# A two-layer transformer trunk on one core: the second exchange of hidden blocks is issued behind the third weight load of the next up projection

## The reference

```python
def squared_relu_mlp(x, w1, w2):
    h = jax.nn.relu(x @ w1)
    return (h * h) @ w2
...
        x = layer_norm(ALPHA * x + mix, ln_mix_g[layer], ln_mix_b[layer])
        x = layer_norm(ALPHA * x + squared_relu_mlp(x, mlp_w1[layer], mlp_w2[layer]), ln_mlp_g[layer], ln_mlp_b[layer])
```

## Time and profile before

| what | value |
|---|---|
| runs | 2122.4, 2122.74, 2124.38 us |
| profiled execution: its own time | 2122.97 us |
| its span, first to last instruction | 2121.2 us |
| granted TensorE clock, mean | 0.999 |
| busy: PE, DVE, ACT, POOL | 2098.9, 1596.4, 1055.1, 25.6 us |
| groups `pair_step(0)` to `(5)`, of about 85 us each | from about 474 us (layer 0) and 1551 us (layer 1) |
| HBM read | 406.26 MB, 193 GB/s over the span |

### The profile page before, as it was taken

The page is one execution under the profiler, slowest core; times in us unless marked ns, Lnnn a source line. Parts: engine busy times, 40 slices in busy tenths (PEclk is TensorE's granted clock), DMA queues, the critical chain, the costliest instruction groups (busy, mean ns, idle before and its releaser), DMA issues.

```text
span 2121.2 us, 26630 instructions
## 1 busy us (share of the span) xinstructions
PE 2098.9 (99%) x9860; PEld 1751.8 (83%) x9860; DVE 1596.4 (75%) x1623; ACT 1055.1 (50%) x1196; POOL 25.6 (1%) x38
## 2 busy tenths in 40 slices
PE   9999999999999999999999999999999999999998
PEld 7888887888888888888888888888888888888886
DVE  6766666859788788696687767577686977978876
ACT  5445656435445354453645544555354554544543
POOL 2000000000000000000000000000000000000001
PEclk9999999999999999999999999999999999999999
DMA  9554564666566566666464555554666655656563
GB/s 286 180 177 159 173 244 161 216 217 220 180 213 220 198 209 209 227 227 238 159 220 158 182 177 177 174 185 161 230 203 228 212 195 198 236 196 214 204 228 149
DMA packets 216122, 426.18 MB, mean 201 GB/s; under 512 B 14993, under 2 KB 50049, under 8 KB 215025
## 3 DMA queue, kind: packets, MB, share of 16 engines
q1 hardware_dynamic: 214208, 415.75, 58.1%
q0 software_dynamic: 1840, 9.44, 1.3%
HBM read 406.26 MB, written 2.10 MB: 193 GB/s over the span
## 4 chain that ended last, share of the span: by engine, by line
PE 87%; DVE 3%; SPq 3%; DMA 3%; issue 2%; ACT 1%; POOL 0%; DVEq 0%; POOLq 0%
PE ps L1017 18%; PE ps L1019 17%; PE ps L1018 17%; PE ps L929 10%; PE ps L955 6%; PE ps L957 5%; PE ps L956 5%; PE ps L933 5%; SPq L379 3%; DMA raw<-in_mlp_w 1%; DMA raw<-in_ev_w_in 1%; PE ps L1130 0%; DVE res L1517 0%; DVE w_lo L1926 0%; DVE late L1951 0%
## 5 line engine op out<-in xcount | busy, mean ns | idle before, releaser
L790 ACT ACTIVATE w_hi<-raw 128x1024 fp32r<-128x1024 f32 x284 | 294.9, 1058 | 317.8 <-PE ps L1019 312.6
L1422 DVE TENSOR_TENSOR w_lo<-raw,w_hi 128x1024 fp32r<-128x1024 f32 x264 | 319.6, 1219 | 127.9 <-ACT w_hi L498 127.1
L1919 DVE TENSOR_TENSOR w_lo<-raw,w_hi 128x1024 fp32r<-128x1024 f32 x284 | 342.5, 1219 | 88.9 <-ACT w_hi L790 88.7
L498 ACT ACTIVATE w_hi<-raw 128x1024 fp32r<-128x1024 f32 x256 | 267.5, 1056 | 170.4 <-PE ps L957 113.8
L1017 PE MATMUL ps<-w_hi,yT 128*128 128x512 f32 x812 | 316.3, 390 | 0.0
L1019 PE MATMUL ps<-w_hi,yT 128*128 128x512 f32 x812 | 316.0, 389 | 0.0
L1018 PE MATMUL ps<-w_lo,yT 128*128 128x512 f32 x812 | 315.9, 389 | 0.0
L929 PE MATMUL ps<-xT,w_hi 128*128 128x512 f32 x1016 | 259.0, 396 | 2.1 <-DVE xT L1467 1.0
L929 PEld LDWEIGHTS ps<-xT,w_hi 128*128 128x128 f32 x1016 | 183.1, 188 | 36.7 <-issue 1.5
L1017 PE MATMUL ps<-w_hi,xT 128*128 128x512 f32 x524 | 204.8, 391 | 2.8 <-DVE res L1517 2.4
L1018 PE MATMUL ps<-w_lo,xT 128*128 128x512 f32 x524 | 203.9, 389 | 0.0
(11 more groups left out here) (273 smaller groups left out, 3248.2 us busy)
## 6 DMA issues: line engine op xcount, KB each, us to landing
raw<-in_mlp_w SPq DMA_DIRECT2D x256, 1024.0 KB, 5.2
raw<-in_od_w_in SPq DMA_DIRECT2D x48, 1024.0 KB, 5.1
raw<-in_ev_w_in SPq DMA_DIRECT2D x36, 1024.0 KB, 5.1
raw<-in_ev_w_out SPq DMA_DIRECT2D x16, 1024.0 KB, 5.1
raw<-in_od_w_out SPq DMA_DIRECT2D x16, 1024.0 KB, 5.1
ks<-cross SPq DMA_DIRECT2D x256, 32.0 KB, 1.9
ks<-qs SPq DMA_DIRECT2D x256, 32.0 KB, 1.9
raw<-in_ev_w_in SPq DMA_DIRECT2D x8, 512.0 KB, 8.8
```

What stands on the lines that cost most here:

```text
L498: nc.scalar.activation(flat(w_hi[:, k % NSPL]), flat(raw[:, k % NRAW]), ACT.Copy).then_inc(s_hi, 1)
L790: nc.scalar.activation(slot_part(0, slot, 2), flat(raw[:, k % NRAW]), ACT.Copy).then_inc(s_hi, 1)
L1422: nc.vector.tensor_tensor(flat(w_lo[:, k % NSPL]), flat(raw[:, k % NRAW]), flat(w_hi[:, k % NSPL]).bitcast(F32), ALU.subtract).then_inc(s_ ...
L1919: nc.vector.tensor_tensor(slot_part(1, slot, 2), flat(raw[:, k % NRAW]), slot_part(0, slot, 2).bitcast(F32), ALU.subtract).then_inc(s_lo, 1)
```

## The change

SP's `pair_step` gets a second argument, the number of the load behind which the second exchange is issued. It is 2, so that the exchange stands behind the third load (u = 2) of the up projection, where it stood behind the first (u = 0). For i = 0 it stays 0, and so that call is written out ahead of the loop, which now runs from i = 1. The programs of the other engines are the same.

```diff
--- before.py
+++ after.py
@@ -409,16 +409,17 @@
                         move_hidden(1)
                 down(b0 + 4, 0, 1)
 
-                def pair_step(i):
+                def pair_step(i, move_behind=2):
                     blk = i * PAIR_BLOCKS + (b0 + 2 + PAIR_BLOCKS)
                     for u in range(2 * PAIRS):
                         up_unit(blk, i + 2, u)
-                        if u == 0:
+                        if u == move_behind:
                             sp.wait_ge(s_sq, i * 2 + (h0 + 3))
                             move_hidden(1)
                     down(blk + 2, i + 1, i + 2)
 
-                with sp.Fori(0, PAIRED - 3) as i:
+                pair_step(0, move_behind=0)
+                with sp.Fori(1, PAIRED - 3) as i:
                     pair_step(i)
                 pair_step(PAIRED - 3)
                 for v in range(2 * PAIRS):
```

## The result

| | before | with the change |
|---|---|---|
| median of seven runs | 2122.74 us (2121.7 to 2124.38) | 2115.41 us (2115.32 to 2116.1) |
| profiled execution, its span | 2122.97, 2121.2 us | 2115.41, 2113.6 us |

The ratio is 0.9966 with a 95% interval of 0.9955 to 0.9978: faster by 7.3 us, or 0.34%. The forecast was 2116.5 us in a range from 2115.6 to 2121.0.

What follows compares the result with a forecast made beforehand. PE was taken to bound the kernel, losing 6.1 to 6.6 us in ten stalls behind DVE's late add; with 6.2 taken off, 2122.97 us profiled becomes 2116.8, and the median, 0.23 lower, 2116.5 us, range 2115.6 to 2121.0.

Steps and rivals of the forecast that it cites:

- What bounds, and where the time is lost: PE bounds, busy 2098.9 of 2121.2 us; groups 1 to 5 lose 6.6 us at the first plain_products.
- The cause: DVE's add of block 3 is late: DVE idles 8.42 us for load u = 1, issued behind the exchange.
- One microsecond of lead removes the whole stall: At plain_products: group 0's add, begun at 483.01, ended at 484.23 and its matmul at 485.23 was on its pitch.
- The steps of the changed order: Group 1, layer 0: exchange from 548.1, u = 3 issued 558.6, landed 563.8, add ended 567.3, 2.2 us early.
- The unknown of the sum: Landing time of load u = 3 behind the exchange, bounded by 5.2 and 8.6 us; 5.2 taken.
- B: Rival: load u = 3 lands 8.6 us after issue, add 0.8 us later than now, ten times: 2131 us; 4%.
- C: Rival: exchange lands late behind two 1 MB loads, 9.8 us after last issue, delaying squares: 2123 to 2126 us; 3%.
- Rival A: Reordering only moves the wait to load u = 3, SP's issue time bounds: 2122.7 us, partly 2118 to 2122; 13%.
- 6.1 us (gaps) to 6.6 us (steps of L839) go; I take 6.2: Total gain from PE's stalls in groups 1 to 5 of both layers, by visible gaps or by L839's period.
- The range: Whole kernel: 2115.6 us up into rival A's partial form, 2121.0 us, around the forecast 2116.5.

Runs made afterwards that it cites:

- places 1 to 3: Changed kernel with the second exchange behind load 1, 2 (the change itself) or 3 in groups 1 to 5: 2115.82, 2115.41 and 2115.56 us.
- add_behind_split: Kernel before, with DVE's add of block 3 one instruction later, behind the split of unit 1's sums: 2160.19 us, ratio 1.0174.
- all_groups_2: Kernel before, with the exchange behind the third load (u = 2) in all six groups, group 0 included, no peeled code: 2125.16 us, ratio 1.0011.
- group0_behind_1: Changed kernel with group 0's exchange behind load u = 1 instead of u = 0: 2126.5 us, ratio 1.0018.
- all_groups_2b: The all_groups_2 kernel run once more, unchanged: 2125.82 us, ratio 1.0016; its profiled execution took 2127.81 us.
- behind_4: Changed kernel with the exchange behind the fifth load (u = 4) in groups 1 to 5: 2127.0 us, ratio 1.002.

## Why the prediction was right, and where it was wrong

**What bounds, and where the time is lost: right.** The ten gaps before plain_products are gone, and group 0 had and has none.

**The cause: right in its source, too narrow in its last step.** The source, load u = 1 behind the exchange, is shown by the places 1 to 3, which all free it and all give the same time. But "One microsecond of lead removes the whole stall" is true only if what follows on DVE has that lead too. The add alone, moved by 1.14 us, gave nothing.

**The steps of the changed order: right within a microsecond.** Forecast in the clock of before (0.9 us later than the changed trace): exchange from 548.1, measured 548.2; load u = 3 from 558.6, measured 559.5, because the sixteen issues took 11.0 us and not 10.2; landing 5.2 us, measured 5.0; end of the add 567.3, measured 568.0. The lead was 1.6 us in place of 2.2. The unknown of the sum fell at its lower bound. Rivals B and C did not occur: over the ten groups load u = 3 landed in 4.9 to 5.3 us, and no DMA of the sixteen took more than 5.6 us (4.7 in group 1). That is longer than the 4.3 that the prediction took from the earlier trace rows, but far from the 9.8 that C needs.

**Rival A** did not occur either: the time moved, though the sixteen issues took 11.0 us in place of 10.2. The rule of the Trainium skill ("Perfetto Trace Analysis", What "DMA-bound" means), that a sequencer whose track is solid DMA slices is a bound of its own, does not decide in the way in which I applied it to that stretch: the same issues in another order gave 7.3 us.

**The sum: the step that failed is "6.1 us (gaps) to 6.6 us (steps of L839) go; I take 6.2".** The trace says 6.6: L839's steps were the exact measure, and the count of visible gaps left out about 0.05 us a group in matmuls spaced 0.23 to 0.24 us behind a stall. The prediction had both figures and took the one near the lower without giving a reason. With 6.6 the forecast would have been 2116.1. The same term had a second fault: it took the stalls of one profile for fixed. They vary (6.6, 6.5 and 7.9 us in three executions of the same order, on average 7.0), and they are gone with the change, so the average counts. With 7.0 the forecast would have been 2115.7; three profiles give this average only roughly. Some 0.3 us are then left. Openings vary by more than that between executions, and I cannot assign them.

**The range: its lower end was too near.** It stood 0.9 us below the forecast. Between profiles the openings alone differ by up to 1.0 us (the first L839 or L840 starts at 514.4 to 515.4 in the nine profiles without a stall in group 0), and the stalls of the kernel before by 1.4 us. So a size that was off by so little could carry the time over the edge.

## What to carry to other kernels

Where a queue in order holds urgent loads behind a long run of small issues, find who waits for each item and how long before its need each can be issued: here three of five places were equally good and both neighbours were slow. Look first for the wait at the source of a late chain: here closing DVE's hole gave 7.3 us, and the better of two reorderings behind it 3.0. Measure a repeated stall by the period of an instruction that is bound to the stalled engine, and take the average over executions where the stall depends on transfers.

## What the runs showed of the hardware that was not expected

A stall of PE can cost more than itself. With the granted clock at 1.00 ahead of it, an idle of 2.34 us was followed by 0.50 for some 3 us (`add_behind_split`, matmuls 0.43 us apart in place of 0.227, 1.7 us more). The length of the idle alone does not decide: one group earlier in the same execution an idle of 2.79 us was followed by 1.00. An idle of 3.10 us in `all_groups_2` was followed by 1.00 too, and one of 3.00 us in `group0_behind_1` and one of 3.39 us in `all_groups_2b` by 0.50. The shorter stalls, with idles up to 0.71 us in the kernel before and 1.48 us in `behind_4`, never showed it. Also, sixteen DMA issues of 0.6 us each take between 10.2 and 11.5 us, as one of them may last up to 1.8 us.
